# Two softmax attentions: GpSimd normalizes the second half of each pair, VectorE copies that half's transposed block

## The chip, the core and the metric

The kernel runs on one core of a Trainium2 chip. The metric is device time in microseconds from start to end of one execution; the figure given is the median of several. Its engines are TensorE (PE; PEld is its weight loader), VectorE (DVE), ScalarE (ACT), GpSimd (POOL) and the DMA queues, of which SyncE (SP) issues most. They run side by side, and only semaphores order them against each other.

## The reference

The program is one block of a first model followed by one of a second, over 512 tokens of width 1024. The first block has an RMS norm, an input projection, a stick-breaking attention over 4 heads, a chunked attention with a relative-position bias over 8 heads, a short convolution, an output projection and a SwiGLU layer. The second has an RMS norm, a projection, a convolution branch, a windowed attention of 16 query heads on 4 key heads with a sink, and a product-key expert layer. What matters here are the two softmaxes:

```python
# first block, chunked attention, 8 heads
scores = jnp.where(valid, scores + bias, -jnp.inf)
probs = jax.nn.softmax(scores, axis=-1)
out = jnp.einsum('bhcqk,bhckd->bhcqd', probs, vb)

# second block, windowed attention with a sink, 16 heads
m = jnp.maximum(logits.max(-1), sink_f)
p = jnp.exp(logits - m[..., None])
denom = p.sum(-1) + jnp.exp(sink_f - m)
o = jnp.einsum('bkgqs,bskd->bqkgd', p, vs)
o = o / denom
```

## The kernel before, in words

Every engine has its own program, written out by hand; nothing plans or reorders it. Weights stream from memory in slices of 128 x 1024 through a ring of four buffers. ScalarE rounds each slice to its high part (`high`), GpSimd computes the low part as the difference (`low`), and TensorE multiplies with both.

Both attentions use one scheme, `attention(st)`, written once for each of PE, ACT and DVE, with `st` being `stage1` or `stage2`. The work is cut into pairs. A pair is two heads (the two halves, `half` 0 and 1) by one block of 128 queries. The first attention has 16 pairs, in four groups of four, whose blocks have n = 128, 256, 384 and 512 keys. The second has 32 pairs in eight groups of four, with n = 256, 384, 384 and 256. A group is one pair of heads, so its shapes repeat. The life of pair p goes as follows.

- PE computes the scores of both halves into PSUM (`score`, L1976). Score banks alternate between pairs, so the scores of pair p + 1 wait until the logits of pair p - 1 have been taken (`logit`).
- DVE adds the bias table to the scores, negates them, takes the row minimum and writes to the SBUF tile `pr` (L1278, `logit`). There are three `pr` buffers, so pair p waits for the transposes of pair p - 3 (`turned`).
- In the second attention GpSimd writes one more column, the sink, behind the keys of `pr` (`sinks`, L669, semaphore `sunk`); from pair 3 on it waits for the same transposes.
- ACT takes the exponential in place with its row sum (L824, `probs`).
- DVE takes the reciprocal of both sums (L1288), then multiplies each half of `pr` by it (L1291, `normed`). This stands behind the reductions of pair p + 1 in DVE's order.
- PE transposes each half in blocks of 128 into PSUM banks 6 and 7 (L1989, `turned`); a half waits for its normalization and for the copy of the pair before out of its bank (`turned_sb`).
- ACT copies both transposed halves to the SBUF tile `pT` (L834, `turned_sb`), behind the exponentials of pair p + 2.
- PE multiplies them by V (L2000, `mixed`). When a group is done, ACT copies its result out (L839, `head_out`).

PE's order in one step is the scores of pair p + 1, the transposes of pair p - 2, the products with V of pair p - 3. In the second attention DVE also splits the finished head pairs into high and low parts for the next matrix product (`split_out`, L1190 and L1191), one in every fourth pair from pair 10 to pair 30, six in all; the last two come after the loop.

## Time and profile before

| what | value |
|---|---|
| median of three runs | 2365.34 us (2362.56 to 2367.77) |
| the profiled execution | 2365.04 us |
| its span, first to last instruction | 2363.2 us |
| busy PE / DVE / ACT / POOL | 2309.6 / 1715.6 / 872.1 / 1019.4 us |
| first attention | about 199 to 237 us |
| second attention | about 942 to 1016 us |

The page of the profile gives each engine's busy time over the whole span. TensorE is busy for 98% of it, but the ends of matmuls are modelled, so a busy TensorE is not always one at its peak. The chain that ended last runs over TensorE for 75% of the span and over VectorE for 15%. The two attentions take about 112 us together, so their stretches have to be read by themselves; the rows below come from there, and a few from elsewhere, where an operation or a collision between engines can be seen.

### The profile page before, as it was taken

To read this page: it belongs to the slowest core of one execution; us is meant where nothing else is said; L and a number is where in the kernel's file an instruction comes from. 1 tells how busy PE (TensorE), PEld (TensorE's weight loads), DVE (VectorE), ACT (ScalarE), POOL (GpSimd) and SP (SyncE) were. 2 spreads that over 40 slices of the span, in tenths; PEclk is the share of its full clock that TensorE was granted. 3 is DMA by queue.
4 is the path that set the end of the run, shared out by engine and by line. 5 is a ranking of instruction groups with operands and counts; after the bars stand their busy time and mean duration, and the time that the engine had idled before them with its cause. 6 is when DMAs were issued, how large, how long until landed. Compare 5 with 4: busy or idle time off the path is not lost.

```text
span 2363.2 us, 34880 instructions
## 1 busy us (share of the span) xinstructions
PE 2309.6 (98%) x12272; PEld 1980.0 (84%) x12272; DVE 1715.6 (73%) x3188; ACT 872.1 (37%) x1386; POOL 1019.4 (43%) x1080
## 2 busy tenths in 40 slices
PE   7999999999999999999998899999999999999998
PEld 5885788888888887678898898888899999999998
DVE  5467743332389986867999898588787778888886
ACT  3137222222232243832434455444433333333333
POOL 4530555656655556155541001344455433444440
PEclk9999999999999999999999999999999999999999
DMA  5320223333323323122232467999999989999993
GB/s 170 97 64 28 72 89 98 98 98 105 102 96 98 98 89 112 42 72 84 90 100 88 172 256 265 297 370 320 323 336 333 326 298 315 327 346 332 329 350 126
DMA packets 213107, 437.69 MB, mean 185 GB/s; under 512 B 111760, under 2 KB 116368, under 8 KB 209936
## 3 DMA queue, kind: packets, MB, share of 16 engines
q1 hardware_dynamic: 65376, 235.44, 29.8%
q0 software_dynamic: 39440, 142.10, 16.7%
q10 hardware_dynamic: 108192, 58.92, 8.6%
q8 instruction: 51, 0.84, 0.1%
q14 instruction: 48, 0.39, 0.0%
HBM read 401.81 MB, written 30.41 MB: 183 GB/s over the span
## 4 chain that ended last, share of the span: by engine, by line
PE 75%; DVE 15%; issue 4%; POOL 4%; ACT 1%; DMA 1%; DVEq 0%; POOLq 0%; ACTq 0%; SPq 0%
PE bank L2370 21%; PE bank L1831 16%; PE bank L1833 16%; PE bank L1832 16%; POOL lo L656 3%; DVE ohg L1731 2%; PE bank L1989 1%; DVE lo L1670 1%; PE bank L2000 1%; PE bank L1976 1%; DVE oh L1727 1%; DVE oh L1728 1%; PE bank L2311 1%; DVE idx L1629 1%; DVE scb L1622 1%
## 5 line engine op out<-in xcount | busy, mean ns | idle before, releaser
L656 POOL TENSOR_TENSOR lo<-raw,hi 128x256 fp32r<-128x256 f32 (+1 forms) x740 | 631.4, 885 | 772.2 <-ACT hi L775 553.8
L1831 PE MATMUL bank<-inH,hi 128*128 128x512 f32 (+1 forms) x2112 | 778.1, 368 | 30.0 <-DVE inL L1198 14.7
L1833 PE MATMUL bank<-inH,lo 128*128 128x512 f32 (+1 forms) x2112 | 769.5, 364 | 0.0
L1832 PE MATMUL bank<-inL,hi 128*128 128x512 f32 (+1 forms) x2112 | 769.1, 364 | 0.0
L1831 PEld LDWEIGHTS bank<-inH,hi 128*128 128x128 f32 x2112 | 398.5, 189 | 82.0 <-issue 16.8
L1832 PEld LDWEIGHTS bank<-inL,hi 128*128 128x128 f32 x2112 | 398.9, 189 | 45.0 <-issue 0.2
L1833 PEld LDWEIGHTS bank<-inH,lo 128*128 128x128 f32 x2112 | 398.4, 189 | 42.7
L775 ACT ACTIVATE hi<-raw 128x1024 fp32r<-128x1024 f32 x236 | 248.0, 1056 | 403.9 <-PE bank L1833 389.7
L1146 ACT ACTIVATE hi<-raw 128x1024 fp32r<-128x1024 f32 x204 | 215.6, 1057 | 197.9 <-PE bank L2370 197.8
L711 POOL DMA_INDIRECT rows<-rows_u,expert x128 | 188.9, 1476 | 188.1 <-DVE dots L1773 167.1
L1764 DVE TENSOR_TENSOR lo<-raw,hi 128x1024 fp32r<-128x1024 f32 x208 | 253.3, 1219 | 19.8 <-ACT hi L1146 18.6
L711 POOL DMA_INDIRECT rows<-rows_v,expert x128 | 159.6, 1247 | 223.5 <-DVE acc L1784 182.4
L2370 PE MATMUL bank<-hi,WH 128*128 128x512 f32 x768 | 238.0, 391 | 2.8 <-DVE WL L1758 2.8
L2370 PE MATMUL bank<-hi,WL 128*128 128x512 f32 x768 | 237.5, 390 | 0.0
L2370 PE MATMUL bank<-lo,WH 128*128 128x512 f32 x768 | 237.4, 390 | 0.0
L2370 PEld LDWEIGHTS bank<-lo,WH 128*128 128x128 f32 x768 | 144.2, 188 | 31.3
L2370 PEld LDWEIGHTS bank<-hi,WL 128*128 128x128 f32 x768 | 144.1, 188 | 30.9
L2370 PEld LDWEIGHTS bank<-hi,WH 128*128 128x128 f32 x768 | 142.9, 188 | 27.7 <-DVE WL L1758 3.2
L1784 DVE SCALAR_TENSOR_TENSOR acc<-rows,gate_sp,acc 128x1024 f32<-128x1024 f32 x124 | 160.1, 1291 | 4.2 <-DVE acc L1784 0.5
L1773 DVE CUSTOM_DVE_ANT_0 rows<-h_rep,rows 128x1024 f32<-128x1024 f32 x128 | 154.1, 1219 | 7.1 <-DMA rows<-rows_u,expert 7.1
L1548 DVE SCALAR_TENSOR_TENSOR bank<-u,gn,bank 128x512 f32<-128x512 f32 x224 | 148.2, 753 | 0.0
L1758 DVE TENSOR_TENSOR WL<-bank,WH 128x384 fp32r<-128x384 f32 x128 | 71.4, 558 | 87.1 <-ACT WH L1122 82.3
(331 smaller groups left out, 2759.7 us busy)
## 6 DMA issues: line engine op xcount, KB each, us to landing
raw<-stream SPq DMA_DIRECT2D x440, 512.0 KB
Gd<-gates ACTq DMA_DIRECT2D x32, 768.0 KB
gates<-stage_a ACTq DMA_DIRECT2D x12, 1024.0 KB, 4.5
gates<-stage_b ACTq DMA_DIRECT2D x12, 1024.0 KB, 4.3
tbl<-gqa ACTq DMA_DIRECT2D x8, 384.0 KB, 3.3
A<-spilled POOLq DMA_DIRECT2D x8, 384.0 KB
xT<-x SPq DMA_DIRECT2D x4, 512.0 KB, 9.0
h_rep<-h_tok POOLq DMA_DIRECT2D x16, 128.0 KB
```

The lines of the kernel that those rows point to most:

```text
L656: ins = pool.tensor_tensor(lo[:, r, part], raw[:, r, part], hi[:, r, part].bitcast(F32), ALU.subtract)
L711: pool.indirect_dma_start(rows[r][:, :], None, table, bass.IndirectOffsetOnAxis(expert[:, column:column + 1], 0)).then_inc(row_in[r], 16)
L775: act.activation(hi[:, r % RING, :], raw[:, r % RING, :], ACT.Copy).then_inc(hi_done, 1)
L1146: act.activation(hi[:, i % RING, :], raw[:, i % RING, :], ACT.Copy).then_inc(hi_done, 1)
L1548: done.append(chain.mark(dve.scalar_tensor_tensor(to, *tap(j), d, ALU.mult, ALU.add)))
L1764: dve.tensor_tensor(lo[:, r, :], raw[:, r, :], hi[:, r, :].bitcast(F32), ALU.subtract).then_inc((lo_even, lo_odd)[i % 2], 1)
L1773: dve.tensor_tensor_reduce(out=rows[r][:, :], in0=h_rep[of % 2][:, :], in1=rows[r][:, :], scale=1.0, scalar=0.0, op0=ALU.mult, op1=ALU.add ...
L1784: dve.scalar_tensor_tensor(total[:, :], rows[r][:, :], weight, total[:, :], ALU.mult, ALU.add).then_inc(row_used, 1)
L1831: pe.matmul(bank, wh, xh, start=start, stop=False)
L1832: pe.matmul(bank, wh, xl, start=False, stop=False)
L1833: return pe.matmul(bank, wl, xh, start=False, stop=stop_)
L2370: m = pe.matmul(B[2 * b + half], x[:, w, tok], table[:, r, half * T:(half + 1) * T], start=False, stop=stop and last)
```

## The change

Per pair, the normalization of half 1 moves from VectorE to GpSimd (`normalize`), which waits for the reciprocal on a new semaphore `inverse` and signals `normed_odd`. The copy of half 1's transposed block out of PSUM moves from ScalarE to VectorE, which signals `turned_sb_odd`. VectorE's loop gets one step more; in step p its order is the reductions of pair p, a split where one is due, the reciprocal and half 0 of pair p - 1, the copy of pair p - 2. PE waits on the new semaphores where it waited on the old. GpSimd's weight loop is cut at the first attention to make room for its 16 normalizations, and in the second the 32 sink copies and 32 normalizations alternate.

```diff
@@ -465,8 +465,8 @@
         w_ready = sem("w_ready")
         sb_out = sem("sb_out")
 
-        att = [{n: sem(f"{n}{a}") for n in ("score", "logit", "probs", "normed", "turned",
-                                           "turned_sb", "mixed", "head_out", "sunk")} for a in (1, 2)]
+        att = [{n: sem(f"{n}{a}") for n in ("score", "logit", "probs", "normed", "normed_odd", "turned",
+                                           "turned_sb", "turned_sb_odd", "inverse", "mixed", "head_out", "sunk")} for a in (1, 2)]
         tbl_in = [[sem(f"tbl_in{a}{b}") for b in (0, 1)] for a in (1, 2)]
         y_sb = sem("y_sb")
         y_sq_act = sem("y_sq_act")
@@ -656,22 +656,37 @@
                     ins = pool.tensor_tensor(lo[:, r, part], raw[:, r, part], hi[:, r, part].bitcast(F32), ALU.subtract)
                 ins.then_inc(lo_done, 1)
 
-            def sinks():
+            def normalize(st, v):
+
+                s, w = st["s"], st["pairs"][v]
+                pool.wait_ge(s["inverse"], v + 1)
+                for half in (1,):
+                    pr = st["pr"][:, v % PAIRS_PR, half, :w["n"]]
+                    pool.tensor_scalar(pr, pr, st["sm"][:, v % 2, 4, half:half + 1], None, ALU.mult).then_inc(s["normed_odd"], 1)
+
+            def sink(p, w):
 
                 s = att[1]
-                for p, w in enumerate(pairs2):
-                    if p >= PAIRS_PR:
-
-                        pool.wait_ge(s["turned"], 2 * (p - PAIRS_PR + 1))
-                    else:
-                        pool.wait_ge(s["score"], 1)
-                    less = gn[:, w["sink"]].unsqueeze(2)
-                    pool.tensor_copy(pr2[:, p % PAIRS_PR, :, w["n"]:w["n"] + 1], less).then_inc(s["sunk"], 1)
+                if p >= PAIRS_PR:
+
+                    pool.wait_ge(s["turned"], 2 * (p - PAIRS_PR + 1))
+                else:
+                    pool.wait_ge(s["score"], 1)
+                less = gn[:, w["sink"]].unsqueeze(2)
+                pool.tensor_copy(pr2[:, p % PAIRS_PR, :, w["n"]:w["n"] + 1], less).then_inc(s["sunk"], 1)
 
             for r in range(RING):
                 low(r, r, D)
             first = S_IN2 // RING + ADD_LAG + 1
-            with pool.Fori(1, first) as i:
+            with pool.Fori(1, S_OUT // RING) as i:
+                for r in range(RING):
+                    low(i * RING + r, r, PIECE)
+            for r in range(AHEAD):
+                low(S_OUT + r, r, PIECE)
+            for v in range(len(pairs1)):
+                normalize(stage1, v)
+            low(S_OUT + AHEAD, AHEAD, PIECE)
+            with pool.Fori(S_OUT // RING + 1, first) as i:
                 for r in range(RING):
                     low(i * RING + r, r, PIECE)
             for r in range(RING):
@@ -689,7 +704,11 @@
                     low(i * RING + r, r, PIECE)
             for r in range(AHEAD):
                 low(S_WO + r, r, PIECE)
-            sinks()
+            for p, w in enumerate(pairs2):
+                sink(p, w)
+                if p:
+                    normalize(stage2, p - 1)
+            normalize(stage2, len(pairs2) - 1)
             low(S_WO + AHEAD, AHEAD, PIECE)
             with pool.Fori(S_WO // RING + 1, S_PEER // RING) as i:
                 for r in range(RING):
@@ -829,9 +848,8 @@
                         if v >= 2:
 
                             act.wait_ge(s["mixed"], v - 1)
-                        for half in (0, 1):
-                            act.wait_ge(s["turned"], 2 * v + half + 1)
-                            act.activation(st["pT"][:, v % 2, half, :w["n"]], B[6 + half][:, :w["n"]], ACT.Copy).then_inc(s["turned_sb"], 1)
+                        act.wait_ge(s["turned"], 2 * v + 1)
+                        act.activation(st["pT"][:, v % 2, 0, :w["n"]], B[6][:, :w["n"]], ACT.Copy).then_inc(s["turned_sb"], 1)
                     v = p - 4
                     if v >= 0 and v % TT == TT - 1:
                         w = pairs[v]
@@ -1256,7 +1274,7 @@
             def attention(st, amid=None):
                 s, pairs, sm = st["s"], st["pairs"], st["sm"]
                 n = len(pairs)
-                for p in range(n + 1):
+                for p in range(n + 2):
                     if amid:
                         amid(p)
                     if p < n:
@@ -1281,15 +1299,21 @@
                     k = (p - OUT_LAG) // TT
                     if st is stage2 and p % TT == OUT_LAG % TT and 0 <= k < OUT_SPLITS:
                         split_out(k)
-                    if p >= 1:
+                    if 1 <= p <= n:
                         v = p - 1
                         w, b = pairs[v], v % 2
                         dve.wait_ge(s["probs"], v + 1)
-                        chain(dve.reciprocal(sm[:, b, 4, :], sm[:, b, 2, :]))
-                        for half in (0, 1):
-                            pr = st["pr"][:, v % PAIRS_PR, half, :w["n"]]
-                            ins = dve.tensor_scalar(pr, pr, sm[:, b, 4, half:half + 1], None, ALU.mult)
-                            ins.then_inc(s["normed"], 1)
+                        dve.reciprocal(sm[:, b, 4, :], sm[:, b, 2, :]).then_inc(s["inverse"], 1)
+                        dve.wait_ge(s["inverse"], v + 1)
+                        pr = st["pr"][:, v % PAIRS_PR, 0, :w["n"]]
+                        dve.tensor_scalar(pr, pr, sm[:, b, 4, 0:1], None, ALU.mult).then_inc(s["normed"], 1)
+                    if p >= 2:
+                        v = p - 2
+                        w = pairs[v]
+                        if v >= 2:
+                            dve.wait_ge(s["mixed"], v - 1)
+                        dve.wait_ge(s["turned"], 2 * v + 2)
+                        dve.tensor_copy(st["pT"][:, v % 2, 1, :w["n"]], B[7][:, :w["n"]]).then_inc(s["turned_sb_odd"], 1)
 
 
             x_of = lambda k: xT[:, k, :]
@@ -1983,15 +2007,16 @@
                         w = pairs[v]
                         for half in (0, 1):
                             if v >= 1:
-                                pe.wait_ge(s["turned_sb"], 2 * v + half - 1)
-                            pe.wait_ge(s["normed"], 2 * v + half + 1)
+                                pe.wait_ge(s[("turned_sb", "turned_sb_odd")[half]], v)
+                            pe.wait_ge(s[("normed", "normed_odd")[half]], v + 1)
                             for c in range(0, w["n"], P):
                                 m = pe.transpose(B[6 + half][:, c:c + P], st["pr"][:, v % PAIRS_PR, half, c:c + P], ident)
                             m.then_inc(s["turned"], 1)
                     v = p - 3
                     if v >= 0:
                         w = pairs[v]
-                        pe.wait_ge(s["turned_sb"], 2 * v + 2)
+                        pe.wait_ge(s["turned_sb"], v + 1)
+                        pe.wait_ge(s["turned_sb_odd"], v + 1)
                         if w["group"] >= 2 and v % TT == 0:
                             pe.wait_ge(s["head_out"], w["group"] - 1)
                         nb = w["n"] // P
```

The order on VectorE around the split at pair 10 of the second attention, before (`qk_90` holds the finished heads, `pr_94` the probabilities, `sm_95` the statistics, `tbl_97` the bias table):

```order
L1278 ISA pr_94,sm_95<-bank,tbl_97,gn 128x384 [waits turned2,score2]
L1278 ISA sm_95 128x1
L1278 ISA pr_94,sm_95<-bank,tbl_97,gn 128x384
L1278 ISA sm_95 128x1
L1190 TENSOR_SCALAR inH<-qk_90 128x512 [waits head_out2]
L1191 TENSOR_TENSOR inL<-qk_90,inH 128x512 [waits dve_steps]
L1288 RECIPROCAL sm_95<-sm_95 128x2 [waits probs2,in_part]
L1291 TENSOR_SCALAR pr_94<-pr_94,sm_95 128x384 [waits dve_steps]
L1291 TENSOR_SCALAR pr_94<-pr_94,sm_95 128x384
L1278 ISA pr_94,sm_95<-bank,tbl_97,gn 128x256 [waits turned2,score2]
L1278 ISA sm_95 128x1
```

And after, with `pT_96` the transposed probabilities:

```order
L1296 ISA pr_94,sm_95<-bank,tbl_97,gn 128x384 [waits turned2,score2]
L1296 ISA sm_95 128x1
L1296 ISA pr_94,sm_95<-bank,tbl_97,gn 128x384
L1296 ISA sm_95 128x1
L1208 TENSOR_SCALAR inH<-qk_90 128x512 [waits head_out2]
L1209 TENSOR_TENSOR inL<-qk_90,inH 128x512 [waits dve_steps]
L1306 RECIPROCAL sm_95<-sm_95 128x2 [waits probs2,in_part]
L1309 TENSOR_SCALAR pr_94<-pr_94,sm_95 128x384 [waits inverse2]
L1316 COPY pT_96<-bank 128x256 [waits turned2,mixed2]
L1296 ISA pr_94,sm_95<-bank,tbl_97,gn 128x256 [waits turned2,score2]
L1296 ISA sm_95 128x1
```

One of the two normalizations after each reciprocal is gone, and a copy out of PSUM that waits for transposes stands ahead of each pair's reductions.

The order on GpSimd at the second attention, before, from the last slice of weights ahead of it to the first behind it:

```order
L656 TENSOR_TENSOR lo<-raw,hi 128x256 [waits hi_done]
L656 TENSOR_TENSOR lo<-raw,hi 128x256 x3
L669 COPY pr_94<-gn 128x2 [waits score2] x3
L669 COPY pr_94<-gn 128x2 [waits turned2] x29
L656 TENSOR_TENSOR lo<-raw,hi 128x256 [waits hi_done]
L656 TENSOR_TENSOR lo<-raw,hi 128x256 x3
```

And after, the first of the alternating rows:

```order
L676 COPY pr_94<-gn 128x2 [waits score2] x2
L665 TENSOR_SCALAR pr_94<-pr_94,sm_95 128x256 [waits inverse2]
L676 COPY pr_94<-gn 128x2 [waits score2]
L665 TENSOR_SCALAR pr_94<-pr_94,sm_95 128x384 [waits inverse2]
L676 COPY pr_94<-gn 128x2 [waits turned2]
L665 TENSOR_SCALAR pr_94<-pr_94,sm_95 128x384 [waits inverse2]
L676 COPY pr_94<-gn 128x2 [waits turned2]
```

From the third sink copy on, each has a normalization ahead of it in the queue.

The order on TensorE in a step of the second attention, the transposes of a pair of 384 keys (`cs` is the identity) and the products with V of the pair before it, before:

```order
L1989 MATMUL bank<-cs,pr_94 128x128 [waits normed2,turned_sb2]
L1989 MATMUL bank<-cs,pr_94 128x128 x2
L1989 MATMUL bank<-cs,pr_94 128x128 [waits normed2,turned_sb2]
L1989 MATMUL bank<-cs,pr_94 128x128 x2
L2000 MATMUL bank<-pT_96,v_91 64x128 [waits turned_sb2]
L2000 MATMUL bank<-pT_96,v_91 64x128 x5
```

And after:

```order
L2013 MATMUL bank<-cs,pr_94 128x128 [waits normed2,turned_sb2]
L2013 MATMUL bank<-cs,pr_94 128x128 x2
L2013 MATMUL bank<-cs,pr_94 128x128 [waits normed_odd2,turned_sb_odd2]
L2013 MATMUL bank<-cs,pr_94 128x128 x2
L2025 MATMUL bank<-pT_96,v_91 64x128 [waits turned_sb_odd2,turned_sb2]
L2025 MATMUL bank<-pT_96,v_91 64x128 x5
```

The matmuls are the same; half 1 waits on semaphores of its own, and the product with V waits for two copies instead of a count on one semaphore.

## Rows read from the trace of the kernel before

**Rows 1.** Stretches: length, busy time of each engine, granted clock, DMA share, GB/s.
```profile
954.92:963.04 8.12, 8.12 (x87) 5.99 (x86) 7.08 (x29) 7.73 (x25) 0.77 (x4) 1.00 0.17 50
963.04:971.46 8.42, 8.27 (x86) 5.96 (x86) 8.00 (x31) 6.99 (x24) 1.03 (x4) 1.00 0.17 48
996.71:1005.14 8.43, 8.28 (x87) 5.95 (x86) 8.02 (x31) 7.55 (x27) 1.03 (x4) 1.00 0.01 2
215.43:223.96 8.53, 8.53 (x79) 5.42 (x78) 8.24 (x33) 7.73 (x26) 0.00 (x0) 1.00 0.22 64
```

**Rows 2.** Timeline of VectorE, one group: start us, us, what, [idle before].
```profile
965.57 0.42 DVE L1190 TENSOR_SCALAR inH<-qk 128x512 fp32r<-128x512 f32 x1
966.03 0.69 DVE L1191 TENSOR_TENSOR inL<-qk,inH 128x512 fp32r<-128x512 f32 x1
966.76 0.17 DVE L1288 RECIPROCAL sm<-sm 128x2 f32<-128x2 f32 x1
966.96 0.75 DVE L1291 TENSOR_SCALAR pr<-pr,sm 128x384 f32<-128x384 f32 x2
967.62 0.48 DVE L1278 CUSTOM_DVE_ANT_0 pr<-bank,tbl,gn 128x256 f32<-128x256 f32 x1
...
968.43 0.16 DVE L1288 RECIPROCAL sm<-sm 128x2 f32<-128x2 f32 x1
...
970.30 0.61 DVE L1291 TENSOR_SCALAR pr<-pr,sm 128x256 f32<-128x256 f32 x2
970.83 0.61 DVE L1278 CUSTOM_DVE_ANT_0 pr<-bank,tbl,gn 128x384 f32<-128x384 f32 x1
...
971.90 0.17 DVE L1288 RECIPROCAL sm<-sm 128x2 f32<-128x2 f32 x1
```

**Rows 3.** The PSUM copy by source line; then VectorE's timeline, first attention.
```profile
L1206 DVE COPY res<-bank x2: 691/691/691, 38.8 to 306.6; 128x512 f32<-128x512 f32 x2
...
214.56 0.69 DVE L1278 CUSTOM_DVE_ANT_0 pr<-bank,tbl1b 128x512 f32<-128x512 f32 x1 [0.46 <-PE bank L1989]
...
215.17 0.69 DVE L1278 CUSTOM_DVE_ANT_0 pr<-bank,tbl1b 128x512 f32<-128x512 f32 x1
...
219.36 0.42 DVE L1278 CUSTOM_DVE_ANT_0 pr<-bank,tbl1a 128x256 f32<-128x256 f32 x1
...
219.70 0.42 DVE L1278 CUSTOM_DVE_ANT_0 pr<-bank,tbl1a 128x256 f32<-128x256 f32 x1
```

**Rows 4.** Timeline of TensorE at three places of the second attention.
```profile
948.13 0.58 PE L1976 MATMUL bank<-inL,inH 64*128 64x256 f32 x2 [0.22 <-DVE sm L1278]
...
967.52 0.85 PE L1989 MATMUL bank<-cs,pr 128*128 128x128 f32 x6
...
1011.83 0.92 PE L1989 MATMUL bank<-cs,pr 128*128 128x128 f32 x6 [0.77 <-ACT pT L834]
```

**Rows 5.** GpSimd: sink copies (ns min/median/max), and two-input operations by form.
```profile
L669 POOL COPY pr<-gn x32: 179/188/419, 943.1 to 1008.5; 128x2 f32<-128x2 f32 x32
...
L686 POOL TENSOR_TENSOR res<-res,c 128x512 f32<-128x512 f32 x6 | 7.7, 1286 | 0.0
```

**Rows 6.** Waits of the second attention: us in total, times, longest.
```profile
PEld bank L1989 <- ACT pT L834: 6.6, 18, 1.0
```

**Rows 7.** Timelines of GpSimd and VectorE where one holds the other.
```profile
18.35 2.40 POOL L656 TENSOR_TENSOR lo<-raw,hi 128x1024 fp32r<-128x1024 f32 x1 [5.21 <-ACT hi L775]
...
18.37 2.67 DVE L1197 TENSOR_SCALAR inH<-xT,gn 128x512 fp32r<-128x512 f32 x1
...
966.35 0.42 POOL L669 COPY pr<-gn 128x2 f32<-128x2 f32 x1 [1.76 <-PE bank L1989]
```

**Rows 8.** Timelines of ScalarE and GpSimd: GpSimd's answer to a semaphore.
```profile
888.35 1.05 ACT L775 ACTIVATE hi<-raw 128x1024 fp32r<-128x1024 f32 x1
...
889.48 0.74 POOL L656 TENSOR_TENSOR lo<-raw,hi 128x256 fp32r<-128x256 f32 x1 [10.16 <-ACT hi L775]
```

## The prediction

> **What bounds the kernel now.** The profiled execution took 2365.04 us, 2363.2 us of it span; the median of the three timed runs is 2365.34 us, so a sum made on the profiled execution stands 0.3 us below the median. The change touches only the two softmax attentions, about 199 to 237 us and 942 to 1016 us. I read the table of stretches first, to see which engine is full there, then VectorE's timeline inside one group, then who waits for whom.
>
> A group is the four pairs that share a head pair; it repeats with the same shapes, so its period is the unit of the sum. In the first attention a group takes 8.53 us and TensorE is busy for all of it. In the second, groups without VectorE's extra split take 8.12 us, all of it TensorE; those with one split of `qk2` take 8.42 or 8.43 us, with TensorE busy 8.27 and VectorE 8.0 [rows 1]. So the first attention, and the start of the second, hang on TensorE, and relief of ScalarE is worth nothing there. The split groups are nearly full on two engines. VectorE's starts in such a group say what its parts occupy [rows 2]: split 1.19 us (965.57 to 966.76), reciprocal 0.20 (966.76 to 966.96), two normalizations of 384 columns 0.66 (966.96 to 967.62) or of 256 columns 0.53 (970.30 to 970.83), two score reductions of 256 columns 0.81 (967.62 to 968.43) or of 384 columns 1.07 (970.83 to 971.90). A group is 2 x 1.07 + 2 x 0.81 + 4 x 0.20 + 2 x 0.66 + 2 x 0.53 + 1.19 = 8.13 us of 8.42; 0.3 us is left.
>
> **The change part by part.**
>
> *VectorE loses one normalization per pair.* Half of 2 x 0.66 + 2 x 0.53 is 1.19 us a group: 6.94 us remain.
>
> *VectorE gains one copy out of PSUM per pair.* No such copy of 256 or 384 columns is in the trace. Two rows bracket it. The copy of 512 columns out of PSUM lasts 691 ns, like the first attention's reduction of that width (0.69 us), so I take that reduction as the copy's double [rows 3]. Its starts lie 0.34 us apart at 256 columns and 0.61 at 512, its durations are 0.42 and 0.69 [rows 3]; midway, 384 columns take 0.48 and 0.56. A group pays between 2 x 0.34 + 2 x 0.48 = 1.64 and 2 x 0.42 + 2 x 0.56 = 1.96 us. I take 1.76, near the lower end, since a reduction that follows need not await the copy, though each copy waits for two semaphores. VectorE's group becomes 8.70 us (8.60 to 8.90), above TensorE's 8.12: VectorE becomes the bound of the split groups, 0.28 us a group above 8.42. Five full periods lie between the six splits: +1.4 us (+0.9 to +2.4).
>
> *The first split.* In the order the copy of pair p - 2 now stands ahead of the reductions of pair p, and it awaits the transposes that those reductions awaited. When TensorE is the bound, everything behind it, the first split included, starts one copy of 256 columns later: +0.35 us. Against this, at the start of the second attention VectorE reaches its next reductions half a 256 pair (0.27 us) earlier while TensorE waits for it (0.22 us at 948.13) [rows 4]. Net +0.1 us (-0.3 to +0.4).
>
> *GpSimd gains 48 normalizations.* It has never done one here. From below, its copy of 2 columns takes 0.19 us; from above, its two-input operation on 512 columns takes 1.29 us, so 0.97 us at 384 by proportion [rows 5]. I take 0.6 us, between them. Until then only the lateness matters. In a split group TensorE starts the transposes of pair 9 at 967.52, 1.95 us after the split began at 965.57 [rows 2, 4]; the second half follows some 0.3 us later, at +2.3. Now: split 1.19, reciprocal 0.20, VectorE's own half 0.33 (+1.72), then GpSimd 0.6 us: +2.3. At 0.97 us it is +2.7 and TensorE slips 0.4 us, which the new 8.70 us of VectorE mostly covers, since TensorE has 0.58 us spare there. Pairs without a split have the same chain 1.19 us earlier. I charge nothing, up to +2 us over six groups in the range. Queued behind GpSimd's normalization is the sink copy of the pair after next, for which ScalarE's exponential waits; it comes at about 0.3 + 0.6 + 0.2 = 1.1 us after the reciprocal, and VectorE's reductions on which that exponential also waits end at 0.33 + 0.4 + 0.5 = 1.2 us. It is hidden, by little. The GpSimd work on the weight stream stays on the same side of the attention and finds its buffers full either way.
>
> *ScalarE loses 48 copies.* It was busy 7.55 of 8.43 us and is off the bound in the groups. What it held up is TensorE's wait for its copies, 6.6 us in 18 waits of the weight loader [rows 6], mostly under running matmuls; the one exposed wait at the end, 0.77 us at 1011.83 [rows 4], is for the first half's copy, which stays on ScalarE behind the same exponential. I give it 0.
>
> *TensorE.* Same matmuls; the products with V carry one more satisfied wait per pair. Between 0 and 0.05 us each, my estimate from the 0.02 to 0.04 us between dependent VectorE rows [rows 2]: in some 30 pairs where TensorE bounds, 0 to 1.5 us; I take 0.5.
>
> *First attention.* VectorE was busy 8.24 of 8.53 us in the group of rows 1, its fullest, where it also prepares the norm roots [rows 1]. It drops four normalizations, 1.19 us again if 128 and 512 columns continue the line of 256 and 384, and gains four copies, 0.21 + 0.34 + 0.48 + 0.61 = 1.64 us by the distances of rows 3: 8.24 + 0.45 = 8.7 us, 0.2 above TensorE, once. The other groups have less beside the pairs and stay under 8.53. +0.2 us (0 to +0.8).
>
> Sum: 1.4 + 0.1 + 0.5 + 0.2 = +2.2 us, so 2365.04 + 2.2 = 2367.2 and, with the 0.3 us to the median, **2367.5 us**. Own range: 2365 to 2371.
>
> **A row and a rule against the change.** GpSimd started a two-input operation at 18.35 us, for 2.40; VectorE's `tensor_scalar` of 512 columns that started at 18.37 lasted 2.67 us, against 0.42 for the one at 965.57, beside an idle GpSimd. The other way round, a sink copy that began behind VectorE's two-input split took 0.42 instead of 0.19 us [rows 2, 5, 7]. Whoever is first holds the other for the whole instruction. "SBUF — State Buffer" of the Trainium skill, "Who interferes with whom", says just this of VectorE's two-port modes and GpSimd ("Issue order, not op shape, decides who blocks"), and the trace agrees. For the new single-input operation, "GPSIMD Engine Reference" in the same skill (section 4.1) calls one-input work "roughly line-rate", which at 384 columns would be nearer 0.4 than 1 us; no row here shows it, and by it the sum would stay as it is.
>
> **The rivals.**
>
> *A. GpSimd gets there first (slower).* Both start on the same reciprocal: VectorE's own half 0.03 to 0.04 us behind its end [rows 2], GpSimd, by its answer to ScalarE, 0.08 us behind (889.40 to 889.48) [rows 8]. The margin is 0.04 us. If GpSimd wins, VectorE's half waits a whole normalization, 0.4 to 0.7 us a pair. At 0.55, a split group becomes 8.70 + 2.2 = 10.9 us (+2.5 x 5 = 12), an unsplit one 8.70 - 1.19 + 2.2 = 9.7 against 8.12 (+1.6 x 2 = 3), a group of the first attention perhaps 0.8 us longer (x 4 = 3): +18 us, 2383. It decides from the point where GpSimd's start leads. Against it stands the order of the two delays. 12%.
>
> *B. GpSimd's normalization is slow (slower).* At 0.97 us or more, sink copies and second-half transposes come late in every split group: another 0.5 to 1 us each on top of the sum, with some in the start: 2370 to 2376, middle 2373. For it: GpSimd's 1.29 us row. 16%.
>
> *C. ScalarE's relief counts (faster).* If the 0.30 us that split groups lose against 8.12 is ScalarE's latency, not VectorE's load, and the copy is cheap, TensorE keeps 8.12: -0.3 x 6 = -1.8, and the exposed wait at the end (-0.8) and half of the start's (-0.5) go too: 2362.2 us. Against it: 8.60 us of VectorE at the least, in any order. 10%.
>
> *D. The engines trade evenly (no change).* The copy costs what the normalization did, because the reduction starts under its tail: 2365.3. Part of the forecast's neighbourhood. 12%.
>
> **How the numbers follow.** Forecast 50%, A 12, B 16, C 10, D 12. A difference under 0.2% (4.7 us) is about what a measurement cannot tell from no change. Faster by more needs more than C offers: 4%. Slower by more (above 2370.1): A's 12, most of B, 13, and 5 of the forecast's upper edge: 30%. Within: 66%. The range of 8 in 10 goes from C to B's far end: 2362.0 to 2376.
>
> **What would show it.** Split groups of about 8.7 us with VectorE busy throughout, unsplit ones and the first attention's all but unchanged; PSUM copies of about 0.42 and 0.56 us; VectorE's first half at 0.35 to 0.42 us (A would show it near 0.9, and a GpSimd row that starts before it); GpSimd's rows around 0.6 us plus what they are held; TensorE's waits in the second attention for VectorE rather than ScalarE. The forecast is wrong if groups without a split lengthen, or if split groups fall to 8.2 us or below.

## The result, and the profile after

The changed kernel is slower: 2376.08 us, median of 5 runs, against 2365.34 us, median of 5 runs of the kernel before beside them. The ratio is 1.0043 with a 95% interval of 1.0025 to 1.0060, or 10.7 us, where the forecast was 2.2 us. The time stands at the very end of the range that was given for 8 in 10 (2362.0 to 2376), and outside the forecast's own range of 2365 to 2371; a slowdown beyond 2370.1 us had been given 30%. The forecast had the direction right and a fifth of the size.

The profiled execution took 2379.44 us (span 2377.2), 14 us more than that of before. The two attentions account for 9.9 us of it. Measured between the same instructions of both kernels:

| stretch | before | after | difference |
|---|---|---|---|
| first attention | 38.82 | 41.20 | +2.38 |
| between the attentions | 702.34 | 702.31 | 0 |
| second attention, to its first split | 23.90 | 25.31 | +1.4 |
| its five periods from split to split | 42.11 | 46.59 | +4.5 |
| its rest | 22.93 | 24.56 | +1.6 |

The other 4 us lie ahead of the first attention and behind the second. There thirteen profiled executions of this case's kernels, with the same code in those parts, scatter by 5 us (start of the first attention at 198.4 to 203.1 us, the part behind the second 1331.5 to 1336.7 us), so I put them down to no edit.

The table of stretches shows a group with a split, and one of the first attention, from one pair of reductions of 512 columns to the next (columns as in [rows 1]):

```profile
983.98:993.30 9.32, 8.34 (x87) 5.97 (x86) 8.61 (x32) 6.47 (x23) 5.66 (x9) 1.00 0.14 44
215.96:225.67 9.71, 9.26 (x88) 5.77 (x86) 8.74 (x34) 6.36 (x21) 4.79 (x5) 1.00 0.19 56
```

The second attention's group grew from 8.42 to 9.32 us. No engine fills it: TensorE is busy 8.34 us, VectorE 8.61, GpSimd 5.66. In the first attention, TensorE was busy for the whole 8.53 us of a group [rows 1]; now it is for 9.26 of 9.71. The three periods between those reductions of 512 columns were 8.47, 8.53 and 8.53 us before, and are 8.61, 9.71 and 8.99 now. A period longer than any engine's work suggests a loop: a chain of operations on several engines in which each waits for the one before and the last starts the first again. So the next view is who waits for whom, at one split. VectorE's timeline, against [rows 2]:

```profile
979.82 0.42 DVE L1208 TENSOR_SCALAR inH<-qk 128x512 fp32r<-128x512 f32 x1
980.27 0.69 DVE L1209 TENSOR_TENSOR inL<-qk,inH 128x512 fp32r<-128x512 f32 x1
981.00 0.17 DVE L1306 RECIPROCAL sm<-sm 128x2 f32<-128x2 f32 x1
981.20 0.42 DVE L1309 TENSOR_SCALAR pr<-pr,sm 128x384 f32<-128x384 f32 x1
981.54 0.42 DVE L1316 COPY pT<-bank 128x256 f32<-128x256 f32 x1
981.87 0.47 DVE L1296 CUSTOM_DVE_ANT_0 pr<-bank,tbl,gn 128x256 f32<-128x256 f32 x1
...
983.50 0.56 DVE L1316 COPY pT<-bank 128x384 f32<-128x384 f32 x1 [0.21 <-PE bank L2013]
```

GpSimd's and TensorE's, same place:

```profile
981.26 1.47 POOL L665 TENSOR_SCALAR pr<-pr,sm 128x384 f32<-128x384 f32 x1 [1.94 <-DVE sm L1306]
982.68 0.18 POOL L676 COPY pr<-gn 128x2 f32<-128x2 f32 x1
```

```profile
982.88 0.52 PE L2013 MATMUL bank<-cs,pr 128*128 128x128 f32 x3 [0.59 <-POOL pr L665]
```

VectorE's own half starts first, at 981.20 us, 0.03 us behind the reciprocal, and takes 0.42 us, as forecast. GpSimd starts at 981.26 and takes 1.47 us, where the forecast took 0.6. TensorE's second-half transposes start 3.06 us after the split began (979.82 to 982.88), not 2.3, having stood idle 0.59 us for GpSimd. The chain of work that sets the end passes right through it (start us, us, what):

```profile
979.90 0.35 DVE inH L1208
...
980.27 0.70 DVE inL L1209
...
981.00 0.18 DVE sm L1306
981.18 0.09 issue
981.26 1.48 POOL pr L665
982.74 0.14 issue
982.88 0.52 PE bank L2013 x3
983.39 0.59 PE bank L2025 x8
983.98 0.72 PE bank L2000 x6
984.70 0.82 PE bank L2013 x6
...
985.61 0.06 DVE pT L1316
985.67 0.41 issue
986.08 0.61 DVE pr L1296
```

The two reductions that end at 979.89 come round again at 989.21, and every step between them is in the chain. GpSimd by form (busy us, mean ns, idle before):

```profile
L665 POOL TENSOR_SCALAR pr<-pr,sm 128x384 f32<-128x384 f32 x20 | 29.4, 1471 | 19.1 <-DVE sm L1306 18.6
L665 POOL TENSOR_SCALAR pr<-pr,sm 128x256 f32<-128x256 f32 x20 | 21.6, 1080 | 24.6 <-DVE sm L1306 24.6
...
L665 POOL TENSOR_SCALAR pr<-pr,sm 128x512 f32<-128x512 f32 x4 | 7.3, 1824 | 1.4 <-DVE sm L1306 1.2
```

And the waits of the second attention:

```profile
ACT pr L843 <- POOL pr L676: 12.6, 9, 1.9
...
PEld bank L2013 <- ACT pT L852: 4.0, 9, 1.1
PE bank L2013 <- POOL pr L665: 3.9, 7, 0.6
```

ScalarE's exponential now waits 12.6 us in nine places for the sink copy, which stands behind the normalization on GpSimd. The forecast had found it "hidden, by little". In the split groups it still is: their chain goes from GpSimd's normalization to TensorE, and the sink copy stands in the chain only once, at the start of the second attention (951.05 us). The wait of [rows 6] fell from 6.6 us in 18 to 4.0 in 9, and that bought nothing.

### The profile page after: what moved, and what is told of

The parts are those of the page before. It is cut to its first block, busy times and chain, and to the rows that moved or that the text cites. A ratio compares the mean times of both kernels' runs of the same rounds, so it can differ in the third digit from the quotient of the medians.

```text
span 2377.2 us, 34961 instructions
## 1 busy us (share of the span) xinstructions
PE 2313.8 (97%) x12272; PEld 1979.6 (83%) x12272; DVE 1720.7 (72%) x3188; ACT 857.5 (36%) x1338; POOL 1077.9 (45%) x1128
## 4 chain that ended last, share of the span: by engine, by line
PE 71%; DVE 17%; issue 4%; POOL 4%; DMA 2%; ACT 1%; DVEq 0%; POOLq 0%; SPq 0%; ACTq 0%
PE bank L2395 18%; PE bank L1855 16%; PE bank L1857 16%; PE bank L1856 16%; POOL lo L656 3%; DVE ohg L1755 2%; DVE lo L1694 1%; PE bank L2013 1%; DMA Gd<-gates 1%; DVE oh L1751 1%; DVE oh L1752 1%; PE bank L2336 1%; DVE pr L1296 1%; DVE idx L1653 1%; DVE scb L1646 1%
```

## The experiments

Three accounts are held against one another in the expectations. *L*: a loop through GpSimd's slow normalization sets the period. *V*: VectorE's load does. *S*: GpSimd's slowness alone makes the whole loss, and the copy on VectorE adds nothing. A fourth question is how much of GpSimd's time is *hold*, that is, waiting for VectorE, whose own half starts just ahead. Split groups and attentions are read from the profiled execution of each run; the ratios are of timed runs against the kernel before beside them. The fences of each run show the main lines of its edit.

### f1_norm_only: the normalization moves, the copies stay on ScalarE

```diff
-                        act.wait_ge(s["turned"], 2 * v + 1)
-                        act.activation(st["pT"][:, v % 2, 0, :w["n"]], B[6][:, :w["n"]], ACT.Copy).then_inc(s["turned_sb"], 1)
+                        for half in (0, 1):
+                            act.wait_ge(s["turned"], 2 * v + half + 1)
+                            act.activation(st["pT"][:, v % 2, half, :w["n"]], B[6 + half][:, :w["n"]], ACT.Copy).then_inc(s["turned_sb"], 1)
```

> Only the normalization of half 1 moves to GpSimd; both copies stay on ScalarE. Theory L (a loop through GpSimd's slow normalization): a split group is 9.32 us of the changed kernel less the two copies that stood on the loop (0.47 and 0.35), so 8.5 us, and the second attention grows by about 1 us over before; GpSimd's rows stay at 1.08 us (256 columns) and 1.47 (384). Rival V (VectorE's load alone): VectorE has 6.94 us of work a group, so it is at or below before's 8.42. Rival S (GpSimd's slowness alone makes all of it): a split group stays near 9.3 us and the run near 2375 us.

VectorE's copy is gone from its loop, TensorE waits for ScalarE's as before, and VectorE's reciprocal also waits for GpSimd's normalization of two pairs earlier.

Measured: 2372.53 us, ratio 1.0026 (1.0013 to 1.0038); split group 9.02 us; both attentions +5.9 us. VectorE is busy 7.00 us of that group, so its load is not the bound. Neither L (8.5 us) nor S (9.3) had the period: the two copies that L took off the loop are not simply gone, since the sink copy and ScalarE's exponentials and copies stand in the chain instead. The chain goes through GpSimd, then its sink copy, then ScalarE:

```profile
987.94 1.47 POOL pr L665
989.41 0.28 POOL pr L676
...
989.72 0.03 ACT pr L843
```

### f2_copy_only: the copy moves, VectorE keeps both normalizations

```diff
+                        for half in (0, 1):
+                            pr = st["pr"][:, v % PAIRS_PR, half, :w["n"]]
+                            ins = dve.tensor_scalar(pr, pr, sm[:, b, 4, half:half + 1], None, ALU.mult)
+                            ins.then_inc(s["normed"], 1)
```

> Only the copy of half 1 moves to VectorE; it normalizes both halves. Rival V: VectorE's split group is 8.13 + 1.66 = 9.8 us of work, an unsplit one 8.6, so the second attention grows by about 5 x 1.4 + 2 x 0.5 = 8 us and the first by 1 to 3: slower than before by 9 to 11 us, as slow as the full change. Rival S: near before, at most +2 us. Theory L agrees with V here, as no GpSimd stands in the loop; the two part at the runs with GpSimd.

Measured: 2375.49 us, ratio 1.0050 (1.0031 to 1.0070); split group 9.71 us; both attentions +12.85 us.

```profile
976.55:986.26 9.71, 8.51 (x89) 5.97 (x87) 9.50 (x35) 6.57 (x22) 0.74 (x5) 1.00 0.14 42
```

VectorE is busy 9.50 of 9.71 us: here load is the bound. So S falls. In the attentions the copy alone costs more than the whole change, and moving the normalization as well gives 2.95 us back (12.85 to 9.90). The timed ratios, 1.0050 and 1.0043 with intervals that overlap, do not tell the two apart.

### f3_gp_short: GpSimd normalizes 128 columns only

```diff
-                    pr = st["pr"][:, v % PAIRS_PR, half, :w["n"]]
+                    pr = st["pr"][:, v % PAIRS_PR, half, :P]
```

> The changed kernel, but GpSimd normalizes only the first 128 columns of half 1 (the rest stays unnormalized): its rows fall to about 0.65 us. Theory L: 0.4 to 0.8 us leave the loop, and the split group falls from 9.32 to VectorE's load, 8.6 to 8.7 us; the second attention keeps about +2 us over before, the first under +1: some 2368 us. Rival V: nothing changes, 9.3 us a group and 2376. Rival S: the group falls to 8.4, as before.

Measured: 2370.87 us, ratio 1.0020 (1.0009 to 1.0030); GpSimd's rows 0.79 us; both attentions +2.72 us. The group is 8.67 us, and the chain is VectorE's alone:

```profile
978.21:986.89 8.68, 8.29 (x86) 5.97 (x85) 8.46 (x33) 6.46 (x22) 3.71 (x8) 1.00 0.15 47
```

V as the only account falls with it, since it gave 9.3 us here too. This is close to the kernel that the forecast described. Its 8.70 us per split group and +2.2 us came out as 8.67 and +2.7, with less in the second attention (+1.53) and more in the first (+1.19). Timed, the interval is +2.1 to +7.1 us.

### f4, g8 and g11: GpSimd's own pace

All three leave out the normalization of half 0, so VectorE has no operation of its own beside GpSimd's, and 7.05 us of work in a group. TensorE waits for the reciprocal there instead. Against the changed kernel, f4_gp_unheld:

```diff
-                        dve.wait_ge(s["inverse"], v + 1)
-                        pr = st["pr"][:, v % PAIRS_PR, 0, :w["n"]]
-                        dve.tensor_scalar(pr, pr, sm[:, b, 4, 0:1], None, ALU.mult).then_inc(s["normed"], 1)
```

> The changed kernel without VectorE's normalization of half 0 (it is left out), so nothing holds GpSimd's port when its own begins. If the 1.47 us of 384 columns hold 0.35 us of waiting for VectorE, the row falls to 1.12, and 256 columns from 1.08 to 0.80; if GpSimd is simply that slow, they stay at 1.47 and 1.08. Theory L: the loop loses 0.35 us of holding and 0.32 of VectorE's own half, so 8.6 to 8.7 us a group; rival V: VectorE's work falls by 1.19 to 7.4 us and TensorE's 8.12 is the group.

g8_gp_immediate, on top of it:

```diff
-                    pool.tensor_scalar(pr, pr, st["sm"][:, v % 2, 4, half:half + 1], None, ALU.mult).then_inc(s["normed_odd"], 1)
+                    pool.tensor_scalar(pr, pr, 0.5, None, ALU.mult).then_inc(s["normed_odd"], 1)
```

> As f4_gp_unheld (GpSimd's normalization with VectorE's own half left out), but GpSimd multiplies the second half by the constant 0.5 in place of the reciprocal's column (so that half is not normalized; VectorE's half is not either). If the pointer operand makes GpSimd slow, its rows at 384 columns fall from 1.257 us towards 0.5; if the stream of one tensor sets its pace, they stay within 0.1 us of 1.257 and the group stays at about 9.1 us.

g11_gp_two_inputs_unheld, on top of f4 too:

```diff
+                    inverse = st["sm"][:, v % 2, 4, half:half + 1].broadcast_to([P, w["n"]])
+                    pool.tensor_tensor(pr, pr, inverse, ALU.mult).then_inc(s["normed_odd"], 1)
```

> As f4_gp_unheld (VectorE's half is not normalized), with GpSimd's normalization as a multiplication of two tensors. The pace of the form by itself: at 384 columns about 1.06 us by the rows of two inputs at 256 and 512 columns, against 1.257 us of the one-input form; the group then falls from 9.09 us to about 8.9. If both forms run at one pace, 1.257 and 9.09 stay.

Measured, GpSimd's rows by form, in that order:

```profile
L665 POOL TENSOR_SCALAR pr<-pr,sm 128x384 f32<-128x384 f32 x20 | 25.1, 1257 | 20.1 <-DVE sm L1306 19.9
```

```profile
L665 POOL TENSOR_SCALAR pr<-pr 128x384 f32<-128x384 f32 x20 | 23.4, 1171 | 20.7 <-DVE sm L1306 20.7
```

```profile
L666 POOL TENSOR_TENSOR pr<-pr,sm 128x384 f32<-128x384 f32 x20 | 16.5, 827 | 25.5 <-DVE sm L1307 25.5
```

| | GpSimd, 384 columns | split group | group less GpSimd |
|---|---|---|---|
| f4 | 1.257 | 9.09 | 7.83 |
| g8 | 1.171 | 9.01 | 7.84 |
| g11 | 0.827 | 8.66 | 7.83 |
| after | 1.471 | 9.32 | 7.85 |

The group is 7.83 us plus GpSimd's operation, within 0.02 us, from 0.83 to 1.47 us and with VectorE's load at 7.05 or 8.6 us. That is account L, shown by its slope; VectorE's load adds nothing to it. Not all of L's numbers held: for f4 it gave 8.6 to 8.7 us, because it put the hold at 0.35 us and counted VectorE's own half in the loop. The period of 9.09 us shows that this half is not in it. The hold costs 0.21 us at 384 columns (1.471 against 1.257). f1 shows the same within one run: its rows that start together with VectorE's half take 1.47 us, and those that find it done (980.19 + 0.42 us against 980.63) take 1.24:

```profile
980.63 1.24 POOL L665 TENSOR_SCALAR pr<-pr,sm 128x384 f32<-128x384 f32 x1
```

Timed, f4 took 2370.65 us, ratio 1.0018 (1.0008 to 1.0029); g8 (2377.29 us) and g11 (2370.69) were timed once each, so only their rows and periods are used. The pointer operand makes 0.09 us of the 1.257 (g8). The two-input form is the faster one, at 0.827 us below the 1.06 expected of it.

### g5_after_split_late: the changed kernel, its split behind the PSUM copy

```diff
-                    k = (p - OUT_LAG) // TT
-                    if st is stage2 and p % TT == OUT_LAG % TT and 0 <= k < OUT_SPLITS:
-                        split_out(k)
                     if 1 <= p <= n:
...
                         dve.tensor_copy(st["pT"][:, v % 2, 1, :w["n"]], B[7][:, :w["n"]]).then_inc(s["turned_sb_odd"], 1)
+                    k = (p - OUT_LAG) // TT
+                    if st is stage2 and p % TT == OUT_LAG % TT and 0 <= k < OUT_SPLITS:
+                        split_out(k)
```

> The changed kernel with the split of the attention moved in VectorE's order behind its PSUM copy of the same step, so that the row sum's reciprocal of the earlier pair is no longer queued behind that split. Theory L (the group's loop runs through VectorE's reciprocal, GpSimd's 1.47 us and back to TensorE): the split still stands ahead of the next step's reciprocal, so the loop shortens only in part: 0.20 + 0.33 + 0.35 of copies, 1.19 of split, 0.81, 0.20, 1.47 on GpSimd, then the transposes: 9.0 to 9.1 us per group of three pairs in place of 9.32, some 1.5 us less over the second attention. If only the split's place ahead of GpSimd cost the time, the group falls to VectorE's load, 8.7 us. If it was load alone, it stays at 9.3.

Measured: 2371.97 us, ratio 1.0024 (1.0011 to 1.0038); the group 8.94 us, the second attention 3.8 us shorter than the changed kernel's.

```profile
976.77:985.71 8.94, 8.46 (x88) 5.96 (x84) 8.56 (x32) 6.57 (x23) 5.90 (x9) 1.00 0.15 46
```

GpSimd's operation still takes 1.47 us, but it is no longer in the loop. From one split to the next the chain runs over VectorE, ScalarE and TensorE only:

```profile
978.00 0.48 DVE pr L1296
...
978.59 0.37 ACT pr L843
...
979.68 0.38 ACT pT L852
...
980.11 0.55 PE bank L2013 x3
```

The expectation by L had kept GpSimd in it, so that its 9.0 to 9.1 us came near is luck. What is shown is that the place of the split, ahead of the reciprocal that GpSimd waits for, is part of the loss. VectorE is busy 8.56 of 8.94 us. The gain, 0.38 us a group, is a little more than expected, and less than the 8.7 us of load alone would give. (A group is four pairs; the "three" of the expectation is a slip.)

### g10_gp_two_inputs: the changed kernel with the faster form on GpSimd

The edit is g11's, made to the changed kernel.

> The changed kernel with GpSimd's normalization written as a multiplication of two tensors (the second half and its reciprocal's column repeated along the row) in place of the one-input operation with a pointer. GpSimd's rows of two inputs stand at 0.84 us for 256 columns and 1.29 us for 512, so about 1.06 at 384 unheld, some 1.27 with the 0.2 us that VectorE's own half holds it, in place of 1.47. Theory L: each microsecond of GpSimd's operation is one of the group, 9.32 falls to about 9.1 us, 1.2 to 2 us less in all. If VectorE's load or the split's place alone set the time, 9.32 stays. If the form doesn't matter to GpSimd's pace, 1.47 stays and so does 9.32.

Measured: 2389.69 us, ratio 1.0106 (1.0089 to 1.0122), the slowest of all; split group 10.78 us. None of the outcomes expected came. VectorE's and GpSimd's timelines of one pair, and two stretches, each a group:

```profile
1006.50 1.09 DVE L1310 TENSOR_SCALAR pr<-pr,sm 128x384 f32<-128x384 f32 x1
```

```profile
1006.55 0.82 POOL L666 TENSOR_TENSOR pr<-pr,sm 128x384 f32<-128x384 f32 x1 [2.71 <-DVE sm L1307]
```

```profile
983.57:994.35 10.78, 8.82 (x93) 6.38 (x92) 10.57 (x33) 6.57 (x22) 3.79 (x8) 1.00 0.13 38
1005.13:1015.90 10.77, 8.92 (x78) 6.61 (x75) 10.56 (x33) 6.58 (x22) 3.79 (x8) 0.84 0.14 39
```

GpSimd's operation got faster (0.83 us instead of 1.47, and it is not held: g11's is as long), and VectorE's half now takes 1.09 us instead of 0.42, as the mean of its 20 rows (1.086; at 256 columns 0.807 us instead of 0.354). The hold has changed sides: VectorE pays 2 x 0.67 + 2 x 0.45 = 2.2 us a group, and 8.6 + 2.2 = 10.8. That is rival A's price, 10.9 us, in another kernel, though by the profile's starts GpSimd is not first: VectorE's row still begins 0.05 us ahead of GpSimd's. The granted clock was 1.00 in the first stretch and 0.84 on average in the second, so part of that ran at 1.2 GHz in place of 2.4; TensorE had been idle for 2.42 us of the stretch ahead of it (994.35 to 1005.13, busy 8.36 of 10.78). The period is 10.78 us either way: the clock did not set it.

### g6, g9 and g7: was VectorE's load the bound before?

Edits to the kernel before. g6_before_split_late:

```diff
-                    if st is stage2 and p % TT == OUT_LAG % TT and 0 <= k < OUT_SPLITS:
-                        split_out(k)
                     if p >= 1:
...
                             ins.then_inc(s["normed"], 1)
+                    if st is stage2 and p % TT == OUT_LAG % TT and 0 <= k < OUT_SPLITS:
+                        split_out(k)
```

> The kernel before with the split of its attention moved in VectorE's order behind the normalizations; all else as before. Theory L (where nothing of GpSimd stands in the loop, only the split's place ahead of the reciprocal does): the groups with a split fall from 8.42 us towards the 8.13 of those without one, say 8.15 to 8.2, 1.3 to 1.8 us less in all. If VectorE's load and its waits were the bound there, they stay at 8.42.

g9_before_split_spread, in place of the split:

```diff
+                    if st is stage2 and p % TT == OUT_LAG % TT and 0 <= k < OUT_SPLITS:
+                        dve.wait_ge(s["head_out"], k + 1)
+                        chain(dve.tensor_scalar(inH[:, k, :], qk2[:, k, :], 1.0, None, ALU.mult))
+                    k = (p - OUT_LAG - 1) // TT
+                    if st is stage2 and p % TT == (OUT_LAG + 1) % TT and 0 <= k < OUT_SPLITS:
+                        dve.tensor_tensor(inL[:, k, :], qk2[:, k, :], inH[:, k, :].bitcast(F32), ALU.subtract).then_inc(in_part, 1)
```

> The kernel before with the high part of each split behind the normalizations and the low part a pair later. Theory L: 8.12 to 8.2 us per group with a split, 1.5 to 1.8 us less in all, as VectorE no longer has the whole 1.2 us in one step. If load is the bound the groups stay at 8.42.

g7_before_gp_low, the low part (512 columns, not the 384 of the expectation) on GpSimd behind its sink copy:

```diff
+                    if p % TT == (OUT_LAG + 1) % TT and 0 <= k < OUT_SPLITS:
+                        pool.wait_ge(split_high, k + 1)
+                        pool.tensor_tensor(inL[:, k, :], qk2[:, k, :], inH[:, k, :].bitcast(F32), ALU.subtract).then_inc(in_part, 1)
```

> The kernel before with the low part of six splits (an operation of two inputs, 384 columns) on GpSimd, one per group, where GpSimd has nothing else due; VectorE keeps every normalization. VectorE's work in such a group falls by the 0.7 us of the low part; GpSimd's takes some 1.0 to 1.3 us beside it and nobody in the loop of that pair waits for it. Theory L: TensorE's 8.12 becomes the group, 1.5 to 1.8 us less in all. Against it: GpSimd's read of SBUF holds VectorE's normalizations (up to 0.3 us a group) and the sink's copies come later: then 8.3 to 8.5 us.

| | median us | ratio (95%) | split group | second attention |
|---|---|---|---|---|
| g6 | 2366.73 | 1.0005 (0.9996 to 1.0014) | 8.42 | 88.96 |
| g9 | 2365.00 | 1.0001 (0.9992 to 1.0010) | 8.11 | 86.59 |
| g7 | 2363.55 | 0.9993 (0.9984 to 1.0002) | 8.11 | 87.06 |
| before | 2365.32 | | 8.42 | 88.94 |

```profile
972.75:980.85 8.10, 8.10 (x88) 5.98 (x86) 7.92 (x31) 7.68 (x26) 0.98 (x5) 1.00 0.18 51
```

```profile
975.73:983.84 8.11, 8.11 (x88) 5.99 (x84) 7.34 (x30) 7.65 (x26) 2.30 (x5) 1.00 0.16 51
```

In g9 VectorE does the same work as before (busy 7.92 us, against 8.0 in [rows 1]), and the group is 8.10 us with TensorE busy for all of it. So 8.42 us was not VectorE's load. g6 missed, and its chain says why (start us, us, what):

```profile
982.18 0.75 DVE pr L1288 x2
982.93 0.35 DVE inH L1190
...
983.30 0.70 DVE inL L1191
...
984.03 0.48 DVE pr L1278
...
984.61 0.37 ACT pr L824
```

The split moved, but the reduction of the next pair, for which ScalarE's exponential waits, stands behind it. In before the chain takes the split at 982.49 us, the reciprocal at 983.59, both normalizations to 984.54, then that reduction and the exponential at 985.04: the same operations, in another order. g9 takes the 0.7 us of the low part out of it, and g7 takes them off the engine. Both reach TensorE's floor in the split groups. End to end neither is shown faster than before: g7's interval reaches 1.0002, and g9's (-1.9 to +2.4 us) does not hold the 2.35 us less of its attention. Whether something behind the attention gives that back, or it is the scatter of those parts, stays open; in its one profiled execution they took 1335.9 us against 1332.6.

## Why the prediction was right or wrong, by its steps

- **VectorE's load: right.** PSUM copies of 256 and 384 columns took 0.42 and 0.56 us, its own half 0.35 and 0.42 us, all as forecast. With GpSimd out of the way (f3) the group was 8.67 us against 8.70. But in the changed kernel this load was not the bound.
- **GpSimd's 48 normalizations, "I take 0.6 us": the step that failed.** The mean at 384 columns was 1.47 us, 1.26 unheld and 0.21 of hold. Even the upper bound, 0.97 us by proportion from a two-input operation, was too low. It rested on the belief that one input cannot cost more than two; at 512 columns the two-input row of [rows 5] took 1.29 us and the new operation 1.57, unheld (f4). From 1.08 us at 256 columns to 1.82 at 512 the operation grows by 2.9 ns a column (2.5 unheld, 925 to 1566 ns in f4), on top of about 0.3 us. From this cost the forecast drew the charge of nothing: "TensorE slips 0.4 us, which the new 8.70 us of VectorE mostly covers". At 0.97 us that would have been nearly so (by the table of f4, g8 and g11, an estimate of 7.83 + 0.97 = 8.80 us). What it lacked is that the cover ends: VectorE's reductions depend on TensorE and TensorE on GpSimd, and from about 0.84 us of GpSimd, where 7.83 + 0.84 passes 8.67, all further time adds to the period. The Trainium skill's "GPSIMD Engine Reference", section 4.1, calls one-input work "roughly line-rate"; f4's 1.26 us, against VectorE's 0.42 for the same 384 columns, say otherwise, and the measurement decides.
- **Size.** With GpSimd at 1.47 us a period grows by 0.90 us instead of 0.28, 4.5 us instead of 1.4 over five. Another 3.0 us come from the stretches ahead of the first split and behind the last (forecast: 0.6 with the satisfied wait). With GpSimd short (f3) they grow by 0.3 us only, so nearly all of it is GpSimd's as well. Most of the 1.4 us ahead of the first split is lost in the first pairs of the attention, where the chain passes GpSimd at 949.97 us. The groups without a split that follow, 8.12 and 8.11 us between the same reductions before, take 8.69 and 8.14, so the forecast's "all but unchanged" held for the second only.
- **The first attention: +2.38 us against +0.2.** The change's chain there shows GpSimd at 512 columns:

```profile
220.02 0.08 issue
220.11 1.87 POOL pr L665
221.97 0.14 issue
222.11 0.64 PE bank L2013 x4
```

  With GpSimd short (f3) +1.19 us stay, so half of the growth is not GpSimd's. f2, which has nothing but the copy on VectorE, lengthens this attention by 2.31 us, as much as the whole change, with VectorE busy 9.74 of 9.95 us in its longest period. The forecast had put VectorE's load at 8.7 us in one group (8.74 measured) and the rest under 8.53; all three measured periods grew. How the two causes share the 2.38 us beyond that stays open.
- **ScalarE's relief, 0: not contradicted.** f2 has that relief and is 12.85 us slower in the attentions; no run isolates what the relief is worth.
- **Rival A: refuted for the changed kernel**, with VectorE 0.06 us ahead and its half at 0.42 us. g10 shows its price.
- **Rival B was the mechanism**, and was given 16%; with 0.97 us or more for the operation it stood at 2370 to 2376, middle 2373. The measured 2376.08 us is B's far end, at 1.47 us. That the wide range still reached it is owed to B alone. Rivals C and D fell: no split group stayed at 8.42 us or came down to 8.12.

## What to carry to other kernels

Where an operation moves to another engine, ask first whether its result is in the loop of that stage; once that loop is the longest, as here from 0.84 us of GpSimd on, every nanosecond of the slower engine is one of the period, whatever load is saved. A period that no engine fills (9.32 us beside 8.61 and 8.34) was the mark of such a loop, and a moved stall is found by the order of the chain, not by busy sums: splitting one 1.2 us insertion in two (g9) took the groups to TensorE's floor, while moving it whole (g6) did nothing. In the changed kernel moving it whole (g5) did help, because it took GpSimd's operation out of the loop. An operation that the trace does not show on that engine is bounded by measuring it, not by a neighbour with more inputs.

## What the runs showed of the hardware

- On GpSimd a multiplication by a per-partition scalar took 608, 925, 1257 and 1566 ns at 128, 256, 384 and 512 columns (f4), the same by a constant 533, 850, 1171 and 1490 (g8), and as a multiplication of two tensors, the second a column repeated, 399, 613, 827 and 1039 (g11). Two inputs of this kind were the cheaper form by a third. With a full second tensor the two-input rows of before took longer: 1286 ns at 512 columns (an addition in place, [rows 5]) and 841 at 256 (the subtraction of `low`). Whether the repeated column or the multiplication makes the difference was not tried.
- GpSimd's one-input form was held by VectorE and did not hold it: 0.21 us at 384 columns, where 0.36 us of VectorE's row were still to run. The two-input form held VectorE's `tensor_scalar`, by 0.67 us beside an operation of 0.83, and was not held itself, though its row begins 0.05 us later. In neither case was the hold the whole overlap. The rule that I drew from [rows 7], that whoever is first holds the other, and that the Trainium skill's "SBUF — State Buffer" ("Who interferes with whom") puts as "Issue order, not op shape, decides who blocks", does not cover this pair by the starts that the profile gives. Whether the engines' true order differs from those starts was not tried.
